# Two of seven score tiles of a top-256 search counted on ScalarE by signs

## What is computed

```python
idx_logits = jnp.einsum('bqhd,bsd->bqhs', iq, ikeys).astype(jnp.float32) * (IDX_DIM ** -0.5)
score = jnp.einsum('bqhs,bqh->bqs', jax.nn.relu(idx_logits), iw.astype(jnp.float32))
admissible = (k_pos[None, :] // CHUNK) <= (q_pos[:, None] // CHUNK)
score = jnp.where(admissible[None], score, NEG)
_, sel = lax.top_k(score, top_k)
```

## Time and profile before

| | us |
|---|---|
| median of 3 runs | 2078.76 |
| lowest, highest | 2072.36, 2079.02 |
| the profiled execution | 2071.23 |
| its span, first to last instruction | 2069.3 |

### The profile page before, as it was taken

The page is one execution under the profiler, slowest core; times in us unless marked ns, Lnnn a source line. Parts: engine busy times, 40 slices in busy tenths (PEclk is TensorE's granted clock), DMA queues, the critical chain, the costliest instruction groups (busy, mean ns, idle before and its releaser), DMA issues.

```text
span 2069.3 us, 26437 instructions
## 1 busy us (share of the span) xinstructions
PE 1935.9 (94%) x10080; PEld 1549.9 (75%) x10080; DVE 1138.4 (55%) x1700; ACT 637.5 (31%) x1161; POOL 377.6 (18%) x331
## 2 busy tenths in 40 slices
PE   6968999999888986898999989999999999999998
PEld 3533899999433433566994459999999999999997
DVE  1054899999999946776442233333343333433333
ACT  2244322221233126676101122322233222322232
POOL 1101122664477802341000000000000000000000
PEclk9998999999999997999999999999999999999999
DMA  6340112321331253673522223333343333433332
GB/s 204 89 75 20 62 42 76 95 97 57 138 132 61 82 173 96 217 258 149 190 99 92 81 81 111 130 124 122 122 153 122 122 125 131 163 129 122 122 122 101
DMA packets 86606, 242.37 MB, mean 117 GB/s; under 512 B 14549, under 2 KB 32373, under 8 KB 77315
## 3 DMA queue, kind: packets, MB, share of 16 engines
q1 hardware_dynamic: 81643, 227.34, 32.4%
q10 hardware_dynamic: 4896, 14.16, 1.7%
HBM read 211.68 MB, written 26.61 MB: 115 GB/s over the span
## 4 chain that ended last, share of the span: by engine, by line
PE 83%; POOL 5%; DVE 4%; issue 4%; ACT 3%; SPq 1%; DMA 1%; POOLq 0%; DVEq 0%; ACTq 0%
PE ps L642 20%; PE ps L640 20%; PE ps L641 20%; PE ps L966 6%; PE ps L670 4%; PE ps L788 4%; DVE buf L1390 2%; POOL buf L1774 2%; PE ps L863 1%; PE ps L840 1%; POOL buf L1782 1%; PE ps L882 1%; PE ps L823 1%; PE ps L722 1%; PE ps L853 1%
## 5 line engine op out<-in xcount | busy, mean ns | idle before, releaser
L640 PE MATMUL ps<-buf,buf 128*128 128x384 f32 (+2 forms) x2220 | 771.6, 348 | 8.8 <-DVE buf L1339 7.5
L642 PE MATMUL ps<-buf,buf 128*128 128x384 f32 (+2 forms) x2220 | 773.9, 349 | 0.0
L641 PE MATMUL ps<-buf,buf 128*128 128x384 f32 (+2 forms) x2220 | 772.5, 348 | 0.0
L640 PEld LDWEIGHTS ps<-buf,buf 128*128 128x128 f32 x2220 | 418.2, 188 | 28.3 <-DVE buf L1339 5.7
L641 PEld LDWEIGHTS ps<-buf,buf 128*128 128x128 f32 x2220 | 418.5, 188 | 17.9
L642 PEld LDWEIGHTS ps<-buf,buf 128*128 128x128 f32 x2220 | 418.0, 188 | 18.0
L1339 DVE TENSOR_TENSOR buf<-buf,buf 128x1024 fp32r<-128x1024 f32 (+4 forms) x216 | 301.3, 1397 | 176.4 <-ACT buf L1317 39.0
L1641 DVE TENSOR_TENSOR buf<-buf,ps 128x384 f32<-128x384 f32 x66 | 36.6, 555 | 401.6 <-PE ps L642 401.6
L1403 DVE TENSOR_SCALAR_CACHE_REDUCE buf<-buf,buf 128x384 uint8<-128x384 f32 (+6 forms) x231 | 218.3, 1009 | 1.2
L1446 DVE SCALAR_TENSOR_TENSOR buf<-buf,buf,buf 128x1024 f32<-128x1024 f32 x210 | 200.6, 996 | 3.7
L788 PE MATMUL ps<-buf,buf 128*128 128x512 f32 x432 | 193.5, 605 | 4.2 <-DMA buf<-hT_scr 4.2
(11 more groups left out here) (169 smaller groups left out, 1659.3 us busy)
## 6 DMA issues: line engine op xcount, KB each, us to landing
buf<-in_w_ffn SPq DMA_DIRECT2D x67, 1024.0 KB, 5.7
buf<-in_w_ffn SPq DMA_DIRECT2D x66, 512.0 KB, 3.6
buf<-in_cache_k SPq DMA_DIRECT2D x16, 1024.0 KB, 7.5
buf<-in_cache_v SPq DMA_DIRECT2D x16, 1024.0 KB, 10.2
buf<-hT_scr SPq DMA_DIRECT2D x27, 512.0 KB, 3.4
buf<-in_w_cols SPq DMA_DIRECT2D x24, 512.0 KB, 4.4
buf<-in_x SPq DMA_DIRECT2D x18, 512.0 KB, 5.0
gate_scr<-buf ACTq DMA_DIRECT2D x16, 576.0 KB, 5.4
```

Source lines behind the costliest of these rows:

```text
L640: mm(dst, whi, xhi, start=start, stop=False)
L641: mm(dst, whi, xlo, start=False, stop=False)
L642: return mm(dst, wlo, xhi, start=False, stop=stop)
```

## The change

The two longest tiles (1024 and 1152 keys, `signed`) are counted by ScalarE. For each round and tile it runs one activation, Sign of (threshold minus score), whose accumulator gives the number of scores below the threshold minus the number above it. VectorE compares that with L - 512 (`kvec`), in place of the comparison of a count with 256. A score equal to the threshold counts as half, so in these tiles the search can end just below the value that the exact one finds. After the 32 rounds VectorE counts all seven tiles as before, looks in the two for the least score above the threshold (`least`), raises the threshold to it where 256 or more scores are above, and counts the two again.

ScalarE's 32 pairs of activations stand in its stream ahead of its wait for a group of the column stage, at groups 0 to 35, one pair a group and none at every ninth (8, 17, 26, 35). Each pair waits for the threshold of its round (`thr_made`), and VectorE waits for the pair (`signs_made`) before the small steps on the two tiles. VectorE has four small steps a round where it had two. `raised`, a scratch tile, lies where ScalarE's gated-unit results are, so the last step waits until GpSimd has read them (`u_made`).

```diff
--- before.py
+++ after.py
@@ -226,7 +226,11 @@
         flip = place(NSEL, o + 8, I32)
         cnt = take(NSEL, o + 16)
         rest = take(NSEL, o + 24)
-        assert NSEL <= 8 and o + 32 <= o_gmix + D
+        kvec = take(2, o + 32)
+        diff = take(2, o + 40)
+        least = take(2, o + 48)
+        assert NSEL <= 8 and o + 50 <= o_gmix + D
+        signs = place(LS, o_gmix + LS // 2, U8)
         thrf = thr.bitcast(F32)
         hhi = take_r(KD * NTOK, o_w).rearrange("p (k t) -> p k t", k=KD)
         hlo = take_r(KD * NTOK, o_h).rearrange("p (k t) -> p k t", k=KD)
@@ -251,6 +255,7 @@
         us = take(CT * P, o + NTOK).rearrange("p (j t) -> p j t", j=CT)
         uo = take(CH, o + NTOK + CH)
         ut = take(CH, o + NTOK + 2 * CH)
+        raised = take(LS, o_w + CONVO)
         uSamp = uT[:, :, UP:].rearrange("p j (s t) -> p j s t", s=NS)
         cT = uT[:, :, 0:NTOK]
         NLOG = (PB - 2) * H
@@ -384,6 +389,9 @@
             return None if p is None else ("prompt", 2 * p + 1, unit_p[2 * p + 1])
 
 
+        NSIGN = 2
+        signed = list(enumerate(select))[NSEL - NSIGN:]
+
         @block.sync
         def _(sp):
 
@@ -1102,6 +1110,18 @@
             ac(scoreS, bank(5, w=3, n=P), ACT.Copy).then_inc(S("scoreS_copied"), 1)
 
 
+            def sign_step(g):
+
+                step = g - g // 9
+                if g % 9 == 8 or step >= 32:
+                    return
+                act.wait_ge(S("thr_made"), step + 1)
+                for j, (n, (sc, L)) in enumerate(signed):
+                    if step or j:
+                        act.wait_ge(S("signs_made"), NSIGN * step + j)
+                    ac(signs[:, 0:L], sc, ACT.Sign, scale=-1.0, bias=thrf[:, n:n + 1], accum_out=cnt[:, n:n + 1])\
+                        .then_inc(S("signs_made"), 1)
+
             def columns(i, m, glu):
                 t = i * 4 + m
                 e = m % 2
@@ -1110,6 +1130,8 @@
                 if not glu and not (isinstance(t, int) and t < NGLU + 2):
                     act.wait_ge(S(f"gate_out{e}"), (i * 2 + m // 2 - NGLU // 2) * 16)
                 for c in range(NG):
+                    if isinstance(t, int):
+                        sign_step(t * NG + c)
                     act.wait_ge(S("col_done"), t * NG + c + 1)
                     if glu:
                         l = ac((acopy if e else sigb)[:, c], bank(3 * (1 - e) + c, G), ACT.Copy if e else ACT.Sigmoid)
@@ -1395,27 +1417,48 @@
                 dve.wait_ge(S("h_high"), c + 1)
                 low(hlo[:, :, tok(c, G)], hT[:, :, tok(c, G)], hhi[:, :, tok(c, G)]).then_inc(S("h_split"), 1)
 
-            def count(op):
-
-                for n, (sc, L) in enumerate(select):
-                    if n >= 2:
+            def count(op, tiles):
+
+                for j, (n, (sc, L)) in enumerate(tiles):
+                    if j >= 2:
                         ch.wait(1)
-                    ch.add(ve.tensor_scalar(hits[n % 2][:, 0:L], sc, thrf[:, n:n + 1], None, op, ALU.add,
+                    ch.add(ve.tensor_scalar(hits[j % 2][:, 0:L], sc, thrf[:, n:n + 1], None, op, ALU.add,
                                             accum_out=cnt[:, n:n + 1]))
                 ch.wait()
 
+            tiles = list(enumerate(select))
+            own, other = slice(0, NSEL - NSIGN), slice(NSEL - NSIGN, NSEL)
+            for j, (n, (sc, L)) in enumerate(signed):
+                ch.add(ve.memset(kvec[:, j:j + 1], float(L - 2 * TOPK)))
             dve.wait_ge(S("score_done"), NSEL)
-            ch.link(ve.memset(thr, 0))
+            ve.memset(thr, 0).then_inc(S("thr_made"), 1)
+            dve.wait_ge(S("thr_made"), 1)
             for bit in range(31, -1, -1):
-                count(ALU.is_ge)
-                ch.link(ve.tensor_scalar(flip, cnt, float(TOPK), -1.0 if bit == 31 else float(1 << bit),
-                                         ALU.is_lt, ALU.mult))
+                count(ALU.is_ge, tiles[own])
+                value = -1.0 if bit == 31 else float(1 << bit)
+                ch.add(ve.tensor_scalar(flip[:, own], cnt[:, own], float(TOPK), value, ALU.is_lt, ALU.mult))
+                dve.wait_ge(S("signs_made"), NSIGN * (32 - bit))
+                ch.link(ve.tensor_tensor(diff, cnt[:, other], kvec, ALU.subtract))
+                ch.link(ve.tensor_scalar(flip[:, other], diff, 0.0, value, ALU.is_gt, ALU.mult))
                 if bit:
-                    ch.link(ve.scalar_tensor_tensor(thr, thr, 1 << (bit - 1), flip, ALU.bitwise_xor, ALU.bitwise_xor))
+                    ve.scalar_tensor_tensor(thr, thr, 1 << (bit - 1), flip, ALU.bitwise_xor, ALU.bitwise_xor)\
+                        .then_inc(S("thr_made"), 1)
+                    dve.wait_ge(S("thr_made"), 33 - bit)
                 else:
                     ch.link(ve.tensor_tensor(thr, thr, flip, ALU.bitwise_xor))
 
-            count(ALU.is_gt)
+            count(ALU.is_gt, tiles)
+            dve.wait_ge(S("u_made"), 2 * CT)
+            for j, (n, (sc, L)) in enumerate(signed):
+                ch.link(ve.tensor_scalar(raised[:, 0:L], sc, thrf[:, n:n + 1], 3e38, ALU.is_le, ALU.mult))
+                ch.link(ve.tensor_tensor_reduce(raised[:, 0:L], raised[:, 0:L], sc, 1.0, 3e38, ALU.add, ALU.min,
+                                                least[:, j:j + 1]))
+            ch.link(ve.tensor_scalar(diff, cnt[:, other], float(TOPK), None, ALU.is_ge))
+            ch.link(ve.tensor_tensor(least, least, diff, ALU.mult))
+            ch.link(ve.tensor_scalar(diff, diff, 1.0, 3e38, ALU.subtract, ALU.mult))
+            ch.link(ve.tensor_tensor(least, least, diff, ALU.add))
+            ch.link(ve.tensor_tensor(thrf[:, other], thrf[:, other], least, ALU.max))
+            count(ALU.is_gt, tiles[other])
             ch.link(ve.tensor_scalar(rest, cnt, -1.0, float(TOPK), ALU.mult, ALU.add))
             for n, (sc, L) in enumerate(select):
                 if n:
```

## The result

| | before | after |
|---|---|---|
| median of 6 runs each, us | 2077.35 | 2088.24 |
| lowest, highest | 2072.36, 2079.02 | 2085.22, 2091.88 |
| span of the profiled execution | 2069.3 | 2083.7 |

The ratio is 1.0059, with a 95% interval of 1.004 to 1.0078: the changed kernel is slower by 10.9 us in the medians, 14.4 us in the two spans. The runs of one kernel fall in two groups some 6 us apart (before: 2072.4 to 2072.5 and 2076.7 to 2079.0; after: 2085.2 to 2086.5 and 2090.0 to 2091.9), which is why a few us between two single executions say little, and group against group the difference is 13.1 us.

The account below looks back on a forecast made before the run. TensorE and VectorE are full in the column stage, but the end waits for TensorE, then GpSimd's norm, not VectorE's search. A stall of 22 us less 3 given back is +19: 2078.8 + 19 = 2098 us, range 2072 to 2108.

Parts of the forecast that it names:

- The round: VectorE's search round: five shorter tiles' counts of 4.09 us plus small steps, together 4.93, against 7.06 undisturbed before.
- The signs: ScalarE's two Sign activations a round: 1.15 and 1.25 us plus 0.19 per read-out, 2.7 in all, not setting the round.
- The table: Rival: Sign needs another table than Sigmoid, two loads per group, 14 us on top, near 2112; chance 0.03.
- The meetings: VectorE's small steps caught by GpSimd's steps at tile ends, with a wait for a product: 33.0 us in the search.
- The place of the stall: Column stage: TensorE waits for banks that ScalarE empties, in part from group 21 on, most from group 37 to 40.
- the sign named for being right: TensorE idle before line 640 with ScalarE's evacuation as releaser, between 310 and 400 us, 20 us in sum.
- The size of the stall: Column stage: 33.0 us of meetings less 10.3 to spare, so TensorE is held up by 22.7, say 22 us.
- The clock: Rival: TensorE idles in bites between groups 21 and 40; at clock 0.96, 80 us cost 3 more; no chance given.
- After the search: VectorE: exact step 8 us, masks up to 8 more, costing nothing because of more than 70 us of cover.
- The give-back: k and q projections: GpSimd's norm has no taps beside it for some 20 us, gaining 2 to 4 us, taken as 3.
- The sum: Whole kernel: +22 us of stall less 3 given back, +19 us; 2098 on a base of 2078.8.
- nothing changes: From the v projection on: near, bias and mask transfers are issued behind TensorE's progress, not the masks, so no time change.

Follow-up runs that it names:

- the kernel with bites instead: Changed kernel with the eight transposes of the gated unit's last columns, and what hangs on them, moved from behind group 26 to behind group 32; ratio 1.0053.

## Why the prediction was right, and where its steps failed

The direction and the range held: slower, because ScalarE's wait for the threshold holds up TensorE's column stage, by 22.7 us in the forecast and by 23.1 in the trace. Of the mechanism, the coupling and the meetings held; the wait of TensorE that costs the time is another than the one forecast, and that both come to nearly the same number is luck. The median of 2088.24 lies at the very lower edge of the forecast's own 2088 to 2108, and the forecast, 2098, was 10 us too high. By its steps:

- *The round*: 4.93 forecast, 4.80 measured (31 rounds take 180.0 us, of which 31.2 are disturbance). The comparison for the two tiles starts 0.08 us after the one for the five, not behind its end.
- *The signs*: 1.15, 1.25 and 0.19 against 1.149, 1.257 and 0.187. The nearest activation with bias and accumulator was the right row to price a function that the trace did not show.
- *The table*: one load, none between Sign, Sigmoid and Copy behind it. That rival did not come about. The Trainium skill ("ScalarE: Activation LUTs", section on table sets) names relu, copy, identity and abs as functions in every set, and not sign; the trace shows the 64 signs run beside Sigmoid and Copy without a further load, and the first pair, from 222.47 on, even ahead of the stage's load at 225.12.
- *The meetings*: 33.0 forecast with the waits for products, 31.2 measured, and the small steps took 51.2 us where some 21 would do. That GpSimd's start is tied to the threshold is shown by the row at group 5 and by what the split's move took away. The Trainium skill ("SBUF — State Buffer", section "Who interferes with whom") says that a tensor_scalar can take a mode in which it and GpSimd exclude each other for a whole instruction, and that the form that also writes its accumulator can't; the trace agrees, 2.32 against 0.17 for the small step, and for the 384 counts a mean of 0.613 where an undisturbed one takes 0.61.
- *The place of the stall*: wrong. The step that failed is the list of what is queued behind ScalarE's wait. It followed the banks, the weights and the product to the next tile, and stopped there; it did not follow the product of tile 7 to GpSimd's copy and TensorE's transposes behind group 26. That wait had 4.7 us to spare, less than half of the banks' 10.3, and hangs on step 21, ten rounds before the last. So the stall was one of 18.8 us at 335 to 354, released by GpSimd, and not many between groups 37 and 40; the sign named for being right, 20 us of idle time with ScalarE's evacuation as releaser, came to 1.3 us.
- *The size of the stall*: right for a reason partly wrong. By what the run measured, the bank limit alone is 16.7 and not 22.7: the round was 0.13 shorter (4.0 in 31), the search started 0.9 earlier and the meetings cost 1.8 less, and TensorE wanted the bank 0.9 earlier. The missed wait with its clock made up the difference, and that is luck. By the forecast's own numbers the missed wait comes to 22.8 (step 21 at 223.4 + 21 x 4.93, the 20.0 of meetings at groups 2 to 20, and the 10.1 of the chain behind it, less 334.2), so the sum would have been the same had it been seen.
- *The clock*: the rival said 3 us at most, from small bites. One long wait cost 2.3 us behind it; in the kernel with bites instead it was 4.2.
- *After the search*: masks and exact step were to cost 16 us more and cost 35: from the end of the search to the first tap 52.8 before, 87.9 after. The exact step took 17 in place of 8, with four GpSimd meetings of 2.3 to 3.3 us, and the masks took 18 more where up to 8 were forecast (61.5 us in place of 43.7). It cost nothing up to the attention, as the forecast said, because of the cover; the run with more work behind the search shows the same for 23.8 us more. VectorE idles 27.0 and then 38.5 us before the attention:

```profile
774.54 0.29 DVE L1526 CUSTOM_DVE_ANT_0 buf<-ps,buf 128x128 f32<-128x128 f32 x1 [38.48 <-PE ps L848]
```

- *The give-back*: 3 forecast. From the last evacuation to the last projection matmul it is 2.2 (228.8 us before, 226.6 after), and TensorE's waits for the norm fell by 2.4 (24.0 and 21.6); by the norm's own stretch, 3.6. The size was about right.
- *The sum*: +19 forecast up to the last projection, +20.0 in the traces (752.4 becomes 772.4). From there on "nothing changes" failed: the attention took 212.2 us in place of 218.5, and what follows it 0.7 more, so the spans differ by 14.4, and the medians by 10.9. The base was 1.4 us lower and the change 8.1 us smaller than forecast: 4.6 of that are in the traces, all of them behind the last projection, and 3.5 lie between these two executions and the medians. The last section says what is known of the first part.

## What to carry to other kernels

When a wait on another engine's loop is put into an in-order engine that also empties banks, compare two paces first: how often the consumer asks for a step, and how long the loop takes with its disturbances. If it asks faster, the lag grows by the difference each round, and the loss is the lag less the smallest reserve among all waits that hang on this engine, so follow each product to its last reader. When two edits that should each help leave nearly the same loss, look for two limits one behind the other: here only both together paid.

## What the runs showed that was not expected

The attention starts in one of two ways, with the same instructions. The same work from the last projection matmul to the first long reciprocal (line 1470 before, 1513 after) took 47.5 us in the trace before, and 43.1 after. The two stretches of 16 us behind the last projection matmul:

```profile
752.00:768.00 16.00, 10.12 (x29) 5.21 (x28) 5.37 (x26) 6.49 (x18) 3.08 (x12) 0.73 0.75 256
```

```profile
772.00:788.00 16.00, 9.27 (x43) 4.76 (x41) 7.00 (x30) 6.48 (x18) 3.06 (x12) 1.00 0.83 254
```

The first is of the kernel before (granted clock 0.73, 29 matmul records), the second of the one after (1.00, 43). TensorE was full for 54 us and more ahead of both. In the first 4 us TensorE was busy 1.71 us in both; in the next 4 the granted clock was 0.50 in the one and 1.00 in the other. Of the others, the ones with the split moved, with the transposes moved and with both took 43.1 as well, and the whole attention 212.0 to 212.2 us; the rest took 47.3 to 49.3 and 218.4 to 220.3. The run with more work behind the search took the long way with all else as in the changed kernel, so the way doesn't follow the stall. What chooses isn't shown. The distance fits that of the two groups of run times, but the assignment doesn't fit for the kernel before: its profiled execution took the long way and was, at 2071.23, shorter than all six of its runs in the result. So that the changed kernel takes the short way more often isn't shown either, and 8 us of the difference between forecast and result stay open in their cause.

A small step of 128x5 or 128x2 elements pays for nearly the whole instruction of GpSimd that it meets: 2.32 and 2.25 us in place of 0.17, and over the search the small steps took 30 us more than undisturbed ones would, since the loop itself fixes when the two meet. After 18.8 us without work TensorE ran at a granted clock of 0.50, the 1.2 GHz level, and was back at 1.00, the 2.4 GHz level, in the stretch from 361 on.
